# A hybrid decoder layer on one core: routing in two batches, one tile's transposes in the scores' banks, and half of the first expert's gate and up products at the end of the cross-attention

## The chip, the cores and the metric

One core of a Trainium2 chip (trn2) runs the whole program in one launch. The metric is device time in microseconds (us), lower is better. The kernel before has a median of 984.9 us over 3 runs (980.77 to 986.08).

## The reference

One decoder layer over 1024 positions of width 1024: a hybrid token mixer, a cross-attention into 256 memory rows and a grouped mixture of experts, each followed by a LayerNorm of `alpha * x + f(x)`. The change lies between the last two.

```python
def memory_cross_attention(x, mem, wq, wk, wv, wo):      # 4 heads of 128
    q = (x @ wq).reshape(b, s, XA_HEADS, XA_DIM)
    ...
    p = jax.nn.softmax(sc, axis=-1).astype(v.dtype)
    return jnp.einsum('bhsm,bmhd->bshd', p, v).reshape(b, s, XA_W) @ wo

def grouped_moe(x, router_w, router_bias, w_gate, w_up, w_down):
    scores = jax.nn.sigmoid(t @ router_w)                # 16 experts in 4 groups of 4
    biased = scores + router_bias                        # group score: its best two; best group; its best two experts
    ...
    for e in range(N_EXPERTS):
        h = jax.nn.silu(t @ w_gate[e]) * (t @ w_up[e])   # 1024 -> 256
        y = y + combine[:, e:e + 1] * (h @ w_down[e])    # 256 -> 1024
```

## The kernel before, in words

The program is a row of blocks (`project`, `prepare`, `attend`, `cross_attend`, `experts`, and `overflow`, which does work only if an expert is full). In each block every engine has its own hand-written list of instructions; engines wait for each other only by semaphores, and a block ends when all engines have come to its end. The 1024 positions are 8 tiles of 128 rows (NT = 8), and a row of 1024 is turned in KD = 8 pieces of 128.

**cross_attend.** TensorE goes through the tiles t = 0 to 7 in a software pipeline: the queries of tile t (24 products of 512 columns: high and low parts, three each for 8 pieces), in their midst the turned probabilities of tile t-1 (`turn_probs`), then `values(t-1)`, the turned queries, from t = 3 on the turned rows of the normalized tile t-3 (`turn_x2`, into the banks `x_tps`), `scores(t)`, the router's `logits(t-3)` and `outputs(t-1)`, 24 products of 512 columns into `x_acc`. ScalarE (the block `scalar`) copies turned data from the banks back (`xprobT`, `x2T`), takes the exponentials, and the high part of the values (`ohi`); VectorE takes the low part (`olo`), the maxima, the residual and the norm of a tile (`residual`, `norm`), with a reciprocal root from GpSimd between the two.

**Routing.** `rank_experts` makes scores of the logits and ranks the experts of a group, `choose` picks the group and the two experts, `place` (TensorE, a few narrow products) counts how many tokens before a token chose its expert, and `number` makes slot numbers of these counts, a 0/1 matrix `in_first` per tile that says which rows go to expert 0, and the slots for the scatter. It goes in three batches of tiles, `BATCHES`: 0 to 3, 4 and 5, 6 and 7. GpSimd then scatters each tile's rows by two indirect DMAs into `slot_rows` in DRAM (16 in all; that of tile 0 stands ahead of its share in the last tile's norm). For expert 0 the rows are not fetched back: `first_rows(t)` multiplies each tile by `in_first` in TensorE, summed over all 8 tiles in four banks, and ScalarE copies the four banks to `xgT` (`xgT_made`).

**experts.** For each of 16 experts of CAP = 176 slots TensorE multiplies gate and up (two halves m = 0, 1 of 128 hidden columns, gate and up each, 8 products a half and part), turns the next expert's rows (`turn`), and multiplies down (24 products). ScalarE takes the silu, VectorE the product, the high and low parts and the sum with the rows. SyncE waits at the start of the block until all 16 scatters have landed (`rows_scattered`), then fetches the rows of experts 0 and 1 (two DMAs each, of 128 and 48 rows), and then the down weights of expert 1 and the gate and up weights of expert 2. VectorE's list opens with clears, the low part of expert 0's down weights and then, before the first product of expert 0, the slot fields of expert 0's fetched rows (`dve.wait_ge(rows_loaded[0], 32)`).

```python
            sp.wait_ge(k.rows_scattered, 16 * 2 * NT)
            sp.wait_ge(fields_cleared, 2)
            for e in range(2):
                fetch(e * CAP, e)
```

## Time and profile before

| | us |
|---|---|
| median of 3 runs (lowest, highest) | 984.9 (980.77, 986.08) |
| the profiled execution, by its own time | 989.0 |
| its span | 987.2 |
| TensorE busy in the span | 951.2 (96%) |
| VectorE, ScalarE, GpSimd busy | 592.8, 350.8, 196.8 |
| mean granted TensorE clock | 0.986 |

The profile is of one execution, so sums made from its rows stand against 989.0 us, which is 4.1 above the median of the runs. "Busy" of TensorE counts matmuls, whose ends are modelled; weight loads overlap them. In a timeline a line is start, duration, engine, source line, operation and output<-inputs, and in brackets how long the engine stood idle before it and what released it. A matmul in fp32 shows as two instructions (x16 for 8 products). The chain of waits gives for each piece the time from its start to the start of what it released.

### The profile page before, as it was taken

To read this page: it belongs to the slowest core of one execution; us is meant where nothing else is said; L and a number is where in the kernel's file an instruction comes from. 1 tells how busy PE (TensorE), PEld (TensorE's weight loads), DVE (VectorE), ACT (ScalarE), POOL (GpSimd) and SP (SyncE) were. 2 spreads that over 40 slices of the span, in tenths; PEclk is the share of its full clock that TensorE was granted. 3 is DMA by queue.
4 is the path that set the end of the run, shared out by engine and by line. 5 is a ranking of instruction groups with operands and counts; after the bars stand their busy time and mean duration, and the time that the engine had idled before them with its cause. 6 is when DMAs were issued, how large, how long until landed. Compare 5 with 4: busy or idle time off the path is not lost. (4 is left out here: it accounts for less than half of the span.)

```text
span 987.2 us, 15735 instructions
## 1 busy us (share of the span) xinstructions
PE 951.2 (96%) x5687; PEld 805.0 (82%) x5687; DVE 592.8 (60%) x1279; ACT 350.8 (36%) x737; POOL 196.8 (20%) x256
## 2 busy tenths in 40 slices
PE   7999999999999999999999999999999999999995
PEld 6899888677767888788877888889879888888984
DVE  6744341487676776655575554567534476767676
ACT  6123031243376555410024333231232344444342
POOL 0012100121142220012220000004300134343435
PEclk9999999899999999999999999998999999999998
DMA  9122010000699500620116000044788888989872
GB/s 310 56 86 86 1 65 1 1 1 1 234 414 395 182 24 22 211 109 1 52 38 211 3 1 1 1 171 166 266 272 291 270 302 278 314 303 328 305 277 94
DMA packets 67278, 151.60 MB, mean 154 GB/s; under 512 B 8720, under 2 KB 16144, under 8 KB 67216
## 3 DMA queue, kind: packets, MB, share of 16 engines
q1 hardware_dynamic: 59920, 133.82, 38.9%
q0 software_dynamic: 7296, 16.95, 4.5%
q8 instruction: 39, 0.64, 0.2%
q14 instruction: 23, 0.19, 0.1%
HBM read 107.62 MB, written 52.03 MB: 162 GB/s over the span
## 5 line engine op out<-in xcount | busy, mean ns | idle before, releaser
L1970 PEld LDWEIGHTS h_ps<-xgT,e_gate_up 128*128 128x128 f32 x1024 | 155.6, 192 | 4.5 <-issue 2.2
L1970 PE MATMUL h_ps<-xgT,e_gate_up 128*128 128x176 f32 x1024 | 157.1, 315 | 2.2 <-DVEq L2078 2.2
L262 PE MATMUL unit_ps<-whi,xhi 128*128 128x512 f32 (+1 forms) x256 | 98.1, 383 | 6.2 <-DVE wlo L294 6.2
L263 PE MATMUL unit_ps<-wlo,xhi 128*128 128x512 f32 (+1 forms) x256 | 98.0, 383 | 0.0
L264 PE MATMUL unit_ps<-whi,xlo 128*128 128x512 f32 (+1 forms) x256 | 97.9, 383 | 0.0
L262 PEld LDWEIGHTS unit_ps<-whi,xhi 128*128 128x128 f32 x256 | 48.7, 190 | 14.0 <-DVE xlo L338 6.2
L2113 DVE SCALAR_TENSOR_TENSOR z<-y_ps,slot_weight,x_rows 128x512 f32<-128x512 f32 (+1 forms) x64 | 45.6, 746 | 23.7 <-PE y_ps L1984 21.0
L264 PEld LDWEIGHTS unit_ps<-whi,xlo 128*128 128x128 f32 x256 | 48.6, 190 | 7.8
L263 PEld LDWEIGHTS unit_ps<-wlo,xhi 128*128 128x128 f32 x256 | 48.6, 190 | 7.5
L1982 PE MATMUL y_ps<-e_dn_hi,h_hi 128*128 128x512 f32 (+1 forms) x128 | 52.1, 407 | 1.2 <-DVE z L2113 1.1
L1984 PE MATMUL y_ps<-e_dn_hi,h_lo 128*128 128x512 f32 (+1 forms) x128 | 50.2, 392 | 0.0
L1983 PE MATMUL y_ps<-e_dn_lo,h_hi 128*128 128x512 f32 (+1 forms) x128 | 50.1, 391 | 0.0
L2094 DVE TENSOR_TENSOR h<-silu_g,h_ps 128x176 f32<-128x176 f32 x32 | 10.6, 332 | 55.2 <-ACT silu_g L2021 55.2
L2021 ACT ACTIVATE silu_g<-h_ps 128x176 f32<-128x176 f32 x32 | 10.2, 317 | 92.4 <-PE h_ps L1970 85.1
L1026 PE MATMUL o_ps<-prob_T,mla_v 128*64 128x128 f32 x576 | 38.5, 278 | 4.6 <-DVE prob_T L1158 2.2
L1026 PEld LDWEIGHTS o_ps<-prob_T,mla_v 128*64 128x64 f32 x576 | 30.9, 136 | 14.6 <-DVE prob_T L1158 8.8
L2037 ACT ACTIVATE ln_junk<-z,z_neg_mean 128x1024 f32<-128x1024 f32 (+1 forms) x24 | 27.6, 1149 | 41.2 <-DVE z_neg_mean L2068 37.9
L1009 PE MATMUL t_ps<-constants,prob 128*128 128x128 f32 x288 | 41.2, 279 | 0.6 <-DVE prob_T L1158 0.4
L2048 DVE TENSOR_TENSOR e_dn_lo<-e_down_raw,e_dn_hi 128x512 fp32r<-128x512 f32 x64 | 39.7, 677 | 0.8 <-ACT e_dn_hi L2010 0.8
L1082 ACT ACTIVATE prob_T<-t_ps 128x128 f32<-128x128 f32 (+3 forms) x48 | 20.9, 435 | 51.1 <-PE t_ps L1009 51.1
L1158 DVE COPY prob_T<-t_ps 128x512 f32<-128x512 f32 (+3 forms) x48 | 29.7, 619 | 14.0 <-PE t_ps L1009 13.9
L1888 POOL COPY slot_weight<-x_rows 128x2 f32 (+1 forms) x16 | 11.8, 738 | 130.9 <-PE rowsT_ps L1953 66.9
(342 smaller groups left out, 2167.9 us busy)
## 6 DMA issues: line engine op xcount, KB each, us to landing
e_gate_up<-w_gu SPq DMA_DIRECT2D x16, 2048.0 KB, 10.7
e_down_raw<-w_dn SPq DMA_DIRECT2D x16, 1024.0 KB, 5.3
slot_rows<-zeros SPq DMA_DIRECT2D x22, 522.0 KB, 6.3
slot_sums<-zeros SPq DMA_DIRECT2D x22, 512.0 KB, 6.3
x_rows<-slot_rows SPq DMA_DIRECT2D x16, 522.0 KB, 4.5
slot_sums<-z SPq DMA_DIRECT2D x16, 512.0 KB, 4.4
wraw<-w_in SPq DMA_DIRECT2D x24, 256.0 KB, 4.6
xraw<-xT SPq DMA_DIRECT2D x16, 256.0 KB, 5.0
```

The costliest lines, as they stand in the source:

```text
L262: pe.matmul(o, hi, whi[:, s, 0:w], start=(s == 0), stop=False)
L263: pe.matmul(o, hi, wlo[:, s, 0:w], start=False, stop=False)
L264: last = pe.matmul(o, lo, whi[:, s, 0:w], start=False, stop=(s == KD - 1))
L1009: last = pe.transpose(tps[:, j, m * P:(m + 1) * P], prob[:, u % 2, j, m * P:(m + 1) * P], ident)
L1026: last = pe.matmul(ops[r, i % 2, (h // 2) * P:(h // 2 + 1) * P], k.v[:, m, h * MV:(h + 1) * MV], src, start=(m == 0), stop=(m == i))
L1158: dve.tensor_copy(probT[:, v % 2, 0, 0:(z - a) * P], tps[:, 0, 0:(z - a) * P]).then_inc(pT_copied, 1)
L1970: end = pe.matmul(hps[:, m, gu * CAP:(gu + 1) * CAP], gate_up[:, b, s, w], xT[:, s, :], start=(s == 0), stop=(s == KD - 1))
L1982: pe.matmul(out, hi, dn_hi[:, b, w, :], start=(f == 0), stop=False)
L1983: pe.matmul(out, hi, dn_lo[:, b, w, :], start=False, stop=False)
L1984: return pe.matmul(out, lo, dn_hi[:, b, w, :], start=False, stop=(f == 1))
L2048: dve.tensor_tensor(dn_lo[:, b, s, :], dn_raw[:, s, :], dn_hi[:, b, s, :].bitcast(f32), ALU.subtract).then_inc(dn_lo_done, 1)
L2113: dve.scalar_tensor_tensor(z[c][:, f], yps[r, BANK[u], :], wgt[r, b, c:c + 1], rows[b][r, c, f], ALU.mult, ALU.add, accum_out=zsum[r, c, j ...
```

## The change

- The routing goes in two batches, tiles 0 to 4 and 5 to 7. `rank_experts` is cut in two: `score_experts` (scores and bias) and the ranking. For the first batch only the scoring stays before the last tile's `olo`; the ranking comes behind it. GpSimd's scatters are 1, 4 and 3 tiles of two DMAs each, where they were 1, 3, 2 and 2.
- The pass t = 8 of TensorE is written out: `turn_x2(5)` comes ahead of `values(7)` and goes into the scores' banks `x_sps`, `logits(5)` follows, then three quarters of `outputs(7)`, `place(0)`, and the last quarter. ScalarE copies `x2T` of tile 5 before `ohi`.
- `first_rows` are placed anew around `place(1)`; the overflow's count comes before `first_rows(7)`.
- TensorE computes the half m = 0 of expert 0's gate and up (`first_gate`) at the end of the stage, into the banks of `x_tps`, which `experts` now uses as its `h_ps`. The same half is left out behind the block's start.
- SyncE fetches the rows of expert 1 before those of expert 0.

```diff
-    BATCHES = [(0, 4), (4, 6), (6, 8)]
+    BATCHES = [(0, 5), (5, 8)]
...
+                if t == NT - 3:
+                    pe.wait_ge(exps, XH * NT)
+                else:
+                    pe.wait_ge(pT_taken, min(NT, t + 3))
+                bank = sps if t == NT - 3 else tps
...
+            def first_gate():
+                pe.wait_ge(k.gu_loaded[0], 16)
+                for gu in range(2):
+                    for s in range(KD):
+                        if gu == 0 and s % 2 == 0:
+                            pe.wait_ge(k.xgT_made, s // 2 + 1)
+                        last = pe.matmul(tps[:, 0, gu * CAP:(gu + 1) * CAP], k.e_gu[:, 0, s, gu * DE:gu * DE + P], k.xgT[:, s, :],
+                                         start=(s == 0), stop=(s == KD - 1))
+                last.then_inc(k.gu_sum, 1)
...
+            turn_probs(NT - 1)
+            turn_x2(NT - 3)
+            values(NT - 1)
+            logits(NT - 3)
+            outputs(NT - 1, range(0, 3))
+            place(0)
+            outputs(NT - 1, range(3, XH))
             turn_x2(NT - 2)
...
             first_rows(1, range(KD))
+            first_rows(2, range(0, 4))
             turn_x2(NT - 1)
-            first_rows(2, range(0, 4))
+            first_rows(2, range(4, KD))
             logits(NT - 1)
-            first_rows(2, range(4, KD))
-            place(1)
             first_rows(3, range(KD))
             first_rows(4, range(KD))
-            first_rows(5, range(0, 4))
-            place(2)
-            first_rows(5, range(4, KD))
+            place(1)
+            first_rows(5, range(KD))
             first_rows(6, range(KD))
-            first_rows(7, range(KD))
             pe.wait_ge(ov_made, 1)
             pe.matmul(qps[0:1, 480:481], ovsum[:], ones[:, 0:1], start=True, stop=True).then_inc(ov_sum, 1)
+            first_rows(7, range(KD))
+            first_gate()
...
                 if t == NT:
+                    rank_experts(0)
                     choose(0)
...
                 if t == NT - 1:
-                    rank_experts(0)
+                    score_experts(0)
             norm(NT - 1)
+            score_experts(1)
             rank_experts(1)
             choose(1)
             number(1)
-            rank_experts(2)
-            choose(2)
-            number(2)
...
-            scatter(0, [1, 2, 3])
-            scatter(1, [4, 5])
-            scatter(2, [6, 7])
+            scatter(0, [1, 2, 3, 4])
+            scatter(1, [5, 6, 7])
...
-            for e in range(2):
+            for e in (1, 0):
                 fetch(e * CAP, e)
...
-                for m in range(2):
+                for m in range(1 if isinstance(e, int) and e == 0 else 0, 2):
```

TensorE's list behind the turned probabilities of the last tile, before:

```order
L1347 MATMUL x_tps<-constants,xprob 128x128 x8
L1359 MATMUL x_ops<-xprobT,xv 128x128 x8
L1369 MATMUL x_tps<-constants,x_72 128x128 x8
L1380 MATMUL x_qps<-router_w,x2T 128x16 x8
L1392 MATMUL x_sps<-selected_b,up_to 128x64
L1395 MATMUL x_sps<-selected_b,ones 128x48
```

The same place now (`x_72` is the tiles' rows, `xprob` the probabilities, `selected_b` the routing's choice):

```order
L1349 MATMUL x_tps<-constants,xprob 128x128 x8
L1375 MATMUL x_sps<-constants,x_72 128x128 x8
L1361 MATMUL x_ops<-xprobT,xv 128x128 x8
L1386 MATMUL x_qps<-router_w,x2T 128x16 x8
L1415 MATMUL x_acc<-xwo_hi,xoT_hi 128x512
```

The turned rows stand between the probabilities and the values, and 18 of the 24 output products (x_acc) now stand ahead of the place products.

TensorE's list at the end of the stage and the start of `experts`, before:

```order
L1421 MATMUL x_acc<-in_first_expert,x_72 128x176 x2
L1484 MATMUL x_qps<-ones,over_sum 1x1
L1274 UNCONDITIONAL_BRANCH
L1946 UNCONDITIONAL_BRANCH
L1970 MATMUL h_ps<-xgT,e_gate_up 128x176 x32
L1951 MATMUL rowsT_ps<-constants,x_rows_7357 128x128 x8
```

The same place now:

```order
L1428 MATMUL x_acc<-in_first_expert,x_72 128x176 x2
L1446 MATMUL x_tps<-xgT,e_gate_up 128x176 x16
L1275 UNCONDITIONAL_BRANCH
L1968 UNCONDITIONAL_BRANCH
L1992 MATMUL x_tps<-xgT,e_gate_up 128x176 x16
L1973 MATMUL rowsT_ps<-constants,x_rows_7308 128x128 x8
```

Half of the 32 gate and up products of expert 0 have moved ahead of the two branches, which are the end of one block and the start of the next.

VectorE's list where the last tile's low part stands, before:

```order
L1602 TENSOR_SCALAR rank<-rank 128x64
L1603 TENSOR_TENSOR picked<-rank,biased 128x64
L1604 TENSOR_REDUCE group_sum<-picked 128x16
L1666 TENSOR_TENSOR xoT_lo<-x_ops,xoT_hi 128x512
L1585 TENSOR_TENSOR group_beats<-group_sum 128x4x3
```

The same place now (`xoT_lo` is the low part, `beats` and `rank` the ranking):

```order
L1614 TENSOR_SCALAR neg_exp<-neg_exp 128x80
L1615 RECIPROCAL score<-neg_exp 128x80
L1616 TENSOR_TENSOR biased<-score,router_bias 128x80
L1689 TENSOR_TENSOR xoT_lo<-x_ops,xoT_hi 128x512
L1604 TENSOR_TENSOR beats<-biased 128x20x3
```

The ranking has moved from before the low part to behind it, and the batch is 80 columns wide (5 tiles of 16) where it was 64.

## Rows read from the trace of the kernel before

**Rows 1.** Windows: us, PE, PEld, DVE, ACT, POOL busy, clock, DMA share, GB/s.

```profile
659.30:676.20 16.90, 14.68 (x78) 12.41 (x77) 13.62 (x50) 2.83 (x4) 2.03 (x3) 0.80 0.06 23
668.00:672.00 4.00, 4.00 (x10) 3.13 (x11) 3.79 (x9) 0.02 (x1) 0.00 (x0) 0.50 0.02 4
702.30:718.70 16.40, 13.16 (x82) 12.69 (x81) 6.32 (x19) 5.23 (x10) 2.40 (x6) 0.90 0.82 268
718.70:960.00 241.30, 240.18 (x1480) 209.53 (x1480) 151.51 (x322) 96.92 (x201) 69.69 (x90) 1.00 0.87 295
```

**Rows 2.** Chain of waits from the last output products to expert 1's rows.

```profile
674.22 0.24 PE x_acc L1409
...
703.22 4.18 DMA slot_rows<-x,slots
707.42 0.34 SPq L1846
...
708.74 8.21 DMA x_rows<-slot_rows
```

**Rows 3.** Timeline of TensorE (PE), tile 5's logits to expert 1.

```profile
665.47 2.32 PE L1380 MATMUL x_qps<-router_w,x2T 128*128 128x16 f32 x16 [1.11 <-ACT x2T L1498]
...
683.77 1.04 PE L1369 MATMUL x_tps<-constants,x 128*128 128x128 f32 x8
...
685.92 1.96 PE L1380 MATMUL x_qps<-router_w,x2T 128*128 128x16 f32 x16
...
691.63 1.36 PE L1421 MATMUL x_sps<-in_first_expert,x 128*128 128x176 f32 x8
...
694.01 1.36 PE L1421 MATMUL x_sps<-in_first_expert,x 128*128 128x176 f32 x8
...
704.49 11.44 PE L1970 MATMUL h_ps<-xgT,e_gate_up 128*128 128x176 f32 x64 [2.17 <-DVEq L2078]
...
718.64 0.50 PE L1982 MATMUL y_ps<-e_dn_hi,h_hi 128*128 128x512 f32 x1
...
724.31 9.71 PE L1970 MATMUL h_ps<-xgT,e_gate_up 128*128 128x176 f32 x64
```

**Rows 4.** Timeline of VectorE (DVE), routing, norms and the start of experts.

```profile
662.27 0.14 DVE L1595 TENSOR_SCALAR neg_exp<-neg_exp 128x64 f32<-128x64 f32 x1
...
665.41 0.69 DVE L1666 TENSOR_TENSOR xoT_lo<-x_ops,xoT_hi 128x512 fp32r<-128x512 f32 x1
...
668.53 1.28 DVE L1576 SCALAR_TENSOR_TENSOR ln_tmp<-x,ln_mv,ln_g 128x1024 f32<-128x1024 f32 x1
...
673.77 0.16 DVE L1639 TENSOR_SCALAR x<-slots 128x4 f32<-128x4 int32 x1
676.35 1.22 DVE L1565 SCALAR_TENSOR_TENSOR x<-x,x_acc 128x1024 f32<-128x1024 f32 x1 [2.42 <-PE x_acc L1411]
...
680.15 1.28 DVE L1576 SCALAR_TENSOR_TENSOR ln_tmp<-x,ln_mv,ln_g 128x1024 f32<-128x1024 f32 x1 [1.02 <-POOL ln_rs L1750]
...
691.39 0.17 DVE L1595 TENSOR_SCALAR neg_exp<-neg_exp 128x32 f32<-128x32 f32 x1
...
698.24 0.16 DVE L1639 TENSOR_SCALAR x<-slots 128x2 f32<-128x2 int32 x1
...
712.01 0.16 DVE L2051 TENSOR_TENSOR slot_is_high<-x_rows,slot_number 128x2 f32<-128x2 f32 x1 [1.87 <-DMA x_rows<-slot_rows]
...
713.03 0.34 DVE L2096 TENSOR_TENSOR h_lo<-h,h_hi 128x176 fp32r<-128x176 f32 x1 [0.41 <-ACT h_hi L2024]
```

**Rows 5.** Timeline of GpSimd (POOL): scatters and the norm's share.

```profile
674.90 1.24 POOL L1731 DMA_INDIRECT slot_rows<-x,slots  x1 [11.60 <-DVE x L1639]
676.45 0.97 POOL L1731 DMA_INDIRECT slot_rows<-x,slots  x1 [0.30 <-issue]
...
699.20 1.18 POOL L1731 DMA_INDIRECT slot_rows<-x,slots  x1 [2.15 <-DVE x L1639]
```

**Rows 6.** Timeline of SyncE's queue: the load behind the fetches.

```profile
710.23 0.38 SPq L1857 DMA_DIRECT2D e_down_raw<-w_dn  x1
```

More of the change, by code:

```diff
@@ L1366, in turn_x2 @@
                     pe.wait_ge(x2_copied, t)
-                pe.wait_ge(pT_taken, min(NT, t + 3))
+                if t == NT - 3:
[3 more added lines that the diff above has]
+                bank = sps if t == NT - 3 else tps
                 for j in range(KD):
-                    last = pe.transpose(tps[:, j // 4, (j % 4) * P:(j % 4 + 1) * P], x1[:, t, j * P:(j + 1) * P], ident)
+                    last = pe.transpose(bank[:, j // 4, (j % 4) * P:(j % 4 + 1) * P], x1[:, t, j * P:(j + 1) * P], ident)
                 last.then_inc(x2_t, 1)
@@ L1397, in place, with outputs @@
                 last.then_inc(placed, 1)
-            def outputs(t):
+            def outputs(t, parts=range(XH)):
                 pe.wait_ge(o_lo, t + 1)
@@ L1405, in outputs @@
                     pe.wait_ge(taken, t)
-                for s in range(XH):
+                for s in parts:
                     for j in range(2):
@@ L1411, in outputs @@
                         last = pe.matmul(o, olo[:, s, :], k.xwo_hi[:, s, c], start=False, stop=(s == XH - 1))
-                last.then_inc(summed, 1)
+                if parts[-1] == XH - 1:
+                    last.then_inc(summed, 1)
             def first_rows(t, chunks):
@@ L1431, in memory_values @@
                     last.then_inc(v_sum, 1)
+            def first_gate():
[7 more added lines that the diff above has]
+                last.then_inc(k.gu_sum, 1)
             turn(0)
             memory_values(0)
-            for t in range(NT + 1):
-                if t < NT:
-                    queries(t, range(4))
+            for t in range(NT):
+                queries(t, range(4))
                 if t:
                     turn_probs(t - 1)
-                if t < NT:
-                    queries(t, range(4, KD))
+                queries(t, range(4, KD))
                 if t:
@@ L1445, in _ @@
                     memory_values(1, range(0, 1))
-                if t < NT:
-                    turn_queries(t)
+                turn_queries(t)
                 if t == 0:
@@ L1453, in _ @@
                     turn_x2(t - 3)
-                if t < NT:
-                    scores(t)
+                scores(t)
                 if t >= 3:
@@ L1461, in _ @@
                     memory_values(1, range(2, KD))
-                if t == NT:
-                    place(0)
                 if t:
                     outputs(t - 1)
+            turn_probs(NT - 1)
[5 more added lines that the diff above has]
+            outputs(NT - 1, range(3, XH))
             turn_x2(NT - 2)
@@ L1513, in _ @@
                     act.activation(probT[:].rearrange(flat), tps[:].rearrange(flat), ACT.Copy).then_inc(pT_taken, 1)
+                if t == NT:
+                    copy_x2(t - 3)
                 if t < NT:
@@ L1597, in rank_experts @@
                 link(dve.tensor_tensor(bia[:, t, :], score[:, t, :], over(rb[:, None, :], [P, hi - lo, NE]), ALU.add))
+            def rank_experts(n):
+                lo, hi = BATCHES[n]
+                t = slice(lo, hi)
                 v = bia[:, t, :].rearrange("p t (g e) -> p (t g) e", e=EG)
@@ L1800, in experts @@
     dn_hi_done, dn_lo_done = k.sem("dn_hi_done"), k.sem("dn_lo_done")
-    gsum, silu, hmul, hhi_done, hlo_done = k.sem("gu_sum"), k.sem("silu_done"), k.sem("h_mul"), k.sem("hhi_done"), k.sem("hlo_done")
+    gsum, silu, hmul, hhi_done, hlo_done = k.gu_sum, k.sem("silu_done"), k.sem("h_mul"), k.sem("hhi_done"), k.sem("hlo_done")
     ysum, z_made, z_stored, held, held_sp = (k.sem(x) for x in ("y_sum", "z_made", "z_stored", "held", "held_sp"))
@@ L1830, in is_one_of_last @@
         return isinstance(e, int) and e >= NE - count
-    with nc.psum_tensor("rowsT_ps", [P, 3, 512], f32) as tps, nc.psum_tensor("h_ps", [P, 2, 512], f32) as hps, \
+    hps = k.gate_ps
+    with nc.psum_tensor("gate_room", [P, 2, 512], f32), nc.psum_tensor("rowsT_ps", [P, 3, 512], f32) as tps, \
             nc.psum_tensor("y_ps", [P, 3, 512], f32) as yps, nc.Block(no_gpsimd_drain=True) as block:
```

14 lines of the change are left out of this document (8 added, 6 removed).

## The prediction

> **What bounds the kernel now.** I read the windows first: behind the cross-attention TensorE works 240.18 of 241.30 us at full clock [rows 1], so whatever delays it there lasts to the end, and whatever starts it earlier is kept. The two stretches with idle time that the change touches are 659.3 to 676.2 (14.68 of 16.90 busy, mean clock 0.80) and 702.3 to 718.7 (13.16 of 16.40, clock 0.90) [rows 1]. The chain of waits says which one counts. It does not run through TensorE's products just before the second stretch: it comes from VectorE's last slots (made at 698.4), through GpSimd's last four scatters, the last of which starts at 703.22 and lands 4.18 us later, SyncE's four fetch issues from 707.42 on, and 8.21 us until expert 1's rows are there at 716.95 [rows 2, 4, 5]. Then TensorE turns them and starts down at 718.64 [rows 3]. So the number to work out is when down starts; all behind it follows.
>
> **The output products (a gain that does not carry).** Before, TensorE pauses twice for 1.11 us, ahead of values(7) and, as the row shows, ahead of logits(5) [rows 3], and then the clock is granted at 0.50, the lower level (1.2 GHz), while outputs(7) runs [rows 1]: it ends at 676.2. Now the turning of tile 5 (0.9) falls into the first pause, the copy of it lies beside values(7), and the second pause goes. Values(7) starts at 661.4 as before and takes 2.05, logits 1.7: 665.2. With small pauses I expect the clock to hold, so 24 products of 0.23 (one is 0.24 [rows 2]) take 5.5, and place(0), 0.2, stands among them: 671.0, or 5.2 us earlier.
>
> VectorE can't follow. The ranking now stands behind the low part. The low part starts at 664.2, when ScalarE has its high part (1.2 earlier than the 665.41 of before). From it to tile 6's norm VectorE took 668.53 - 665.41 = 3.1, and now the ranking of five tiles on top: scoring and ranking four took 665.41 - 662.27 = 3.1 [rows 4], of which I put 1.0 on the scoring and 2.3 on ranking five. The norm of tile 6 starts at 669.6, 1.1 later. Norm and numbering took 673.93 - 668.53 = 5.4 for four tiles, so 5.7 for five: slots at 675.3, and the last residual there, not at 671.0; before it was at 676.35 [rows 4]. GpSimd took 1.0 us from the slots to tile 0's first scatter and was through with the second at 677.42, 3.5 after the slots [rows 4, 5]. Now that is 678.8, while the variance is ready 2.8 after the residual, at 678.1. So the root waits 0.7 behind the scatters, and the last norm starts at 679.9 against 680.15 [rows 4]. Of 5.2 us some 0.3 is left.
>
> **The second batch.** The last norm takes 2.6 (682.5); TensorE is free then and turns tile 7 at once, where before it came to it at 683.77 [rows 3]. Turning 0.9, half a first_rows (1.2, which covers ScalarE's copy), logits 1.9: VectorE has it at 686.8. A batch of two took 691.39 to 698.40, 7.0 us; one of four 3.1 + 2.5 + 2.7 = 8.3 [rows 4]. Three are 7.7, between the two: slots at 694.5, 3.9 earlier than before. But GpSimd then has six scatters, not four. Before it started 0.8 after the slots and 4.0 lay between the first and the fourth [rows 2, 5]; six make 6.6. Last start 694.5 + 0.8 + 6.6 = 701.9, landed 706.1 against 707.40. **Gain on the chain: 1.3 us**, of 3.9.
>
> **The half of gate and up.** Place(1) waits for nothing new, but first_rows(5) waits for its matrix, 0.8 behind the numbering's start at 692.2: 693.0, a pause of 1.3. Three tiles of 2.4 (694.01 - 691.63 [rows 3]) and the count: 700.4. The half takes 9.71 / 2 = 4.85 [rows 3]: 705.3. The block ends when the last engine does, so this replaces GpSimd's 704.2 as the barrier, and TensorE resumes at 705.6 (before 704.49). That is 0.5 ahead of the landing at 706.1, so SyncE is not held up. The other half takes 4.85, not its share of 11.44: before, after 2.17 idle, the clock fell for the first half [rows 3]. It ends at 710.5.
>
> **The fetches.** They start at 706.2, not 707.42. The first pair (718 KB) took 4.5 us to land when nothing was ahead of it (VectorE went on at 712.01 [rows 4]), the second until 716.95, 9.5 after the first issue. Now expert 1's pair is first: 710.7, turned by 712.4. Expert 0's is second, and VectorE has it ahead of all products of expert 0; before, from landing to h_lo's start took 1.1 and 0.34 for itself [rows 4], so down starts 1.45 after it. When does it land? The issue of the down weights, 1 MB, came 2.8 us after the first fetch's [rows 6]; now ScalarE's split, which follows the block's start, puts it 5.3 after. Bounds for the second pair are thus 6.7 (one DMA more than the first pair, nothing behind it slowing it) and 9.5 (as now). I take 8.0, the middle, since the next load, 2 MB of gate and up weights for expert 2, now goes out right behind the down weights where before it came at 716. Expert 0's rows land at 714.2 and down starts at 715.65, 3.05 earlier than before.
>
> The Trainium skill ("DMA: Bandwidth & Descriptors", section Queues, rings and completion order) says that on each DMA engine descriptors are consumed in ring order. By that the loads issued behind cannot slow the pair, the 9.5 would stay, and down would start at 717.15, 1.5 earlier. The trace does not decide: the second pair's last piece took 8.21 us with the load behind it, though the first pair took 4.5.
>
> **The clock at the new pause.** From 712.4 to 715.65 TensorE has nothing to do, 3.2 us. After 2.17 idle before, the clock fell and the next 64 products took 11.44, not 9.71 [rows 3]: 1.7. I charge 1.55 here, a little less, since part of a fall can lie in the pause. **Sum: 3.05 - 1.55 = 1.5 us earlier.** Against 989.0 of the profiled execution that is 987.5; the median of the runs is 4.1 below, so I forecast 984.9 - 1.5 = 983.4. Bounds: 5.6 gained (second pair after 6.7, ScalarE's silu ready, no fall and 1.2 more from terms above) to 1.5 lost (pair after 9.5 and a fall of 3.0, the cost of the long low stretch in outputs(7), 8.4 where 5.5 is usual).
>
> **Edits of no cost.** The banks shared with `experts` (the first gate waits only for tile 7's copy, 15 us earlier). The gate weights of expert 0 were sent for at the last queries and have long landed. The count ahead of first_rows(7): VectorE has it 0.8 after the slots, at 695.3.
>
> **Rivals.** (a) *The early outputs carry through.* If VectorE's ranking or GpSimd's two scatters cost less than I add up, the last norm follows outputs(7), and 3 to 5 us more come down the chain: 5 us in all at the least, 979.9. For it speaks that both pauses and the low clock go for certain; against it the residual at 675.3, which is VectorE's own sum of work. 0.15. (b) *Nothing reaches down.* By ring order the second pair lands after 9.5, and with the fall of 1.5 the gain is zero: 984.9. For it: expert 0's pair is the one that VectorE needs first, and it has been made second. 0.25. (c) *Slower: the half of gate and up holds the block's end.* TensorE comes to the block's end with 0.5 us of slack. If the pause of 1.3 at 693.0, with the turning and the pauses ahead of it, brings the lower clock, the rest of first_rows and the half lose 1.7 to 3; from 0.5 on the block starts later than the scatters land, the fetches at 707.4 to 708.6, and with the loss of 1.5 behind the fetches nothing is left: 1 to 2.5 slower, 986.4 at the middle. Against it: gate and up ended at 715.9, expert 1's rows came at 716.95, and after that pause of 1.0 the 24 products of down took 724.31 - 718.64 = 5.7, as at full clock [rows 3]. 0.15. That the change does not do what it says is excluded by the lists of instructions.
>
> **The numbers.** My forecast's own case (0.5 to 4.5 gained) has 0.45, (a) 0.15, (b) 0.25, (c) 0.15. The runs of before spread over 5.3 us, so I add 2 us on each side: 978.5 to 987.5 leaves out the far ends of (a) and (c). A difference under 0.5% (4.9 us) is about what a measurement of this kernel can't tell from none. Faster by more takes (a) in full: 0.17. Slower by more takes a shift that no case here has: 0.04. Within: 0.79.
>
> **What the profile after would show.** Outputs(7) at full clock and ended near 671; the last residual near 675.3, released by VectorE's own order and not by TensorE; the last root behind tile 0's scatters; six scatters in a row with the last landing near 706; the first gate's 32 instructions in 4.85; down of expert 0 at about 715.7, held by VectorE's wait for expert 0's rows, and a lower clock behind it. I am wrong if down starts before 714 or after 718, or if the time behind it, 268.5 us from down's start to the span's end, changes by more than 1.

## The result and the profile after

The changed kernel was slower. Over 19 runs of each the medians are 985.96 and 981.4 us, ratio 1.0046 (95% interval 1.0031 to 1.006); 12 later runs gave 1.0014 (0.9996 to 1.0033). The two intervals hardly meet, so a difference of 0.003 between two single ratios is little to build on, and I go by means over all runs where there are several: 986.1 (31 runs of the changed kernel) and 983.4 (193 of before), a loss of 2.7 us. I had forecast 1.5 us less than before. One run of e13 and one of e16 below are left out as outliers (1225.61 and 5446.77 us).

| | before, recorded | before, second trace (e1) | changed |
|---|---|---|---|
| time of the profiled run | 989.0 | 979.2 | 985.9 |
| span | 987.2 | 977.4 | 984.1 |
| mean granted clock | 0.986 | 0.994 | 0.992 |
| last tile's turned probabilities (start) | 659.29 | 655.13 | 655.95 |
| expert 1's gate and up (start) | 724.31 | 716.39 | 721.77 |
| **stretch between the two** | **65.0** | **61.3** | **65.8** |

The start of the stretch differs by 3 to 4 us between the traces although nothing ahead of it was changed; so I compare places by their distance from it, and call the stretch S. TensorE in the changed kernel (timeline: start, duration, what; idle time before it and its releaser in brackets):

```profile
655.95 1.03 PE L1349 MATMUL x_tps<-constants,xprob 128*128 128x128 f32 x8
656.82 1.04 PE L1375 MATMUL x_sps<-constants,x 128*128 128x128 f32 x8
658.10 2.05 PE L1361 MATMUL x_ops<-xprobT,xv 128*128 128x128 f32 x16 [0.24 <-ACT xprobT L1530]
659.99 1.86 PE L1386 MATMUL x_qps<-router_w,x2T 128*128 128x16 f32 x16
...
669.19 1.09 PE L1375 MATMUL x_tps<-constants,x 128*128 128x128 f32 x8 [1.52 <-DVE x L1596]
...
679.38 1.09 PE L1375 MATMUL x_tps<-constants,x 128*128 128x128 f32 x8 [1.13 <-DVE x L1596]
...
690.20 1.46 PE L1428 MATMUL x_sps<-in_first_expert,x 128*128 128x176 f32 x8 [1.46 <-DVE in_first_expert L1655]
...
697.75 4.94 PE L1446 MATMUL x_tps<-xgT,e_gate_up 128*128 128x176 f32 x32
704.26 5.01 PE L1992 MATMUL x_tps<-xgT,e_gate_up 128*128 128x176 f32 x32 [1.57 <-DVEq L2100]
711.00 1.09 PE L1973 MATMUL rowsT_ps<-constants,x_rows 128*128 128x128 f32 x8 [1.73 <-DMA x_rows<-slot_rows]
...
714.58 0.47 PE L2004 MATMUL y_ps<-e_dn_hi,h_hi 128*128 128x512 f32 x1 [1.86 <-issue]
...
721.77 9.71 PE L1992 MATMUL x_tps<-xgT,e_gate_up 128*128 128x176 f32 x64
```

The two pauses of 1.11 ahead of values(7) and logits(5) [rows 3] are 0.24 and none, as meant. But TensorE has six others: three while VectorE is late, one at the block's start, and two ahead of down. And down, 24 products, takes 721.77 - 714.58 = 7.2 us, not 5.7: windows of the changed kernel (the third number from the end is the granted clock):

```profile
709.30:711.00 1.70, 0.00 (x0) 0.00 (x1) 0.61 (x2) 1.18 (x2) 0.00 (x0) 1.00 0.76 209
712.70:714.60 1.90, 0.04 (x2) 0.05 (x1) 1.03 (x5) 0.55 (x2) 0.70 (x3) 1.00 1.03 387
714.60:718.00 3.40, 3.40 (x9) 2.25 (x10) 0.70 (x4) 3.24 (x8) 0.23 (x1) 0.59 0.99 344
```

TensorE idles twice at full clock, and when its work begins, the clock is at the lower level (1.2 GHz) for most of the next 3.4 us. VectorE, GpSimd and SyncE's queue in the changed kernel, their timelines:

```profile
660.89 0.69 DVE L1689 TENSOR_TENSOR xoT_lo<-x_ops,xoT_hi 128x512 fp32r<-128x512 f32 x1 [0.85 <-ACT xoT_hi L1540]
...
672.15 1.21 DVE L1584 SCALAR_TENSOR_TENSOR x<-x,x_acc 128x1024 f32<-128x1024 f32 x1
...
676.72 1.28 DVE L1595 SCALAR_TENSOR_TENSOR ln_tmp<-x,ln_mv,ln_g 128x1024 f32<-128x1024 f32 x1 [1.80 <-POOL ln_rs L1772]
...
683.87 0.19 DVE L1614 TENSOR_SCALAR neg_exp<-neg_exp 128x48 f32<-128x48 f32 x1 [4.54 <-ACT neg_exp L1519]
...
691.52 0.16 DVE L1662 TENSOR_SCALAR x<-slots 128x3 f32<-128x3 int32 x1
...
704.08 0.11 DVE L2099 MEMSET x_rows<- 128x20 f32 x2 [8.56 <-PEq L1275]
...
713.11 0.16 DVE L2073 TENSOR_TENSOR slot_is_high<-x_rows,slot_number 128x2 f32<-128x2 f32 x1 [3.21 <-DMA x_rows<-slot_rows]
```

```profile
674.76 0.97 POOL L1753 DMA_INDIRECT slot_rows<-x,slots  x1 [0.30 <-issue]
675.74 0.28 POOL L1771 TENSOR_SCALAR ln_mv<-ln_mv 128x1 f32<-128x1 f32 x1
...
692.48 1.18 POOL L1753 DMA_INDIRECT slot_rows<-x,slots  x1 [4.63 <-DVE x L1662]
...
699.04 0.96 POOL L1753 DMA_INDIRECT slot_rows<-x,slots  x1 [0.30 <-issue]
```

```profile
704.27 3.22 SPq L1868 DMA_DIRECT2D x_rows<-slot_rows  x4
710.00 0.38 SPq L1879 DMA_DIRECT2D e_down_raw<-w_dn  x1
710.49 0.44 SPq L1882 DMA_DIRECT2D e_gate_up<-w_gu  x1
```

The same places in the second trace of before, an undisturbed run (no low clock anywhere in S), TensorE, VectorE, GpSimd and SyncE:

```profile
661.32 1.96 PE L1380 MATMUL x_qps<-router_w,x2T 128*128 128x16 f32 x16 [1.11 <-ACT x2T L1498]
...
697.71 9.79 PE L1970 MATMUL h_ps<-xgT,e_gate_up 128*128 128x176 f32 x64 [2.17 <-DVEq L2078]
709.07 1.09 PE L1951 MATMUL rowsT_ps<-constants,x_rows 128*128 128x128 f32 x8 [1.58 <-DMA x_rows<-slot_rows]
```

```profile
669.68 1.21 DVE L1565 SCALAR_TENSOR_TENSOR x<-x,x_acc 128x1024 f32<-128x1024 f32 x1
...
674.26 1.28 DVE L1576 SCALAR_TENSOR_TENSOR ln_tmp<-x,ln_mv,ln_g 128x1024 f32<-128x1024 f32 x1 [1.80 <-POOL ln_rs L1750]
...
691.45 0.16 DVE L1639 TENSOR_SCALAR x<-slots 128x2 f32<-128x2 int32 x1
```

```profile
696.43 0.96 POOL L1731 DMA_INDIRECT slot_rows<-x,slots  x1 [0.30 <-POOLq L1274]
```

```profile
700.68 2.40 SPq L1846 DMA_DIRECT2D x_rows<-slot_rows  x4
```

Counted from the start of S, the undisturbed before against the changed kernel: last residual 14.6 and 16.2; last norm 19.1 and 20.8; last slots 36.3 and 35.6; last scatter 41.3 and 43.1; first fetch 45.6 and 48.3; down 55.6 and 58.6; end of S 61.3 and 65.8. Against a run that is not itself disturbed, the new last pass gains nothing and makes the last norm 1.6 later, two batches win 2.4 back (0.8 ahead at the last slots), and the six scatters lose 2.5. The block's start loses 1.0 more, and the low clock 1.5.

One undisturbed trace is the best case of before, as the recorded one is its worst. Seven traces with the old last pass and no filled pauses exist (the two above, e3, e9, e14, e17, e18). Their last residual lies at 14.5 to 14.6 in three, at 15.5 and 15.7 in two, at 17.0 and 17.1 in two; their last scatter starts at 42.4 on average. The changed kernel has 16.2 and 43.1 every time. So against before as it usually runs, the new pass and the two batches together start the last scatter 0.7 later.

### The profile page after: what moved, and what is told of

It is laid out like the page before. It is cut to its first block and busy times, and to the rows that moved or that the text cites. A ratio compares the mean times of both kernels' runs of the same rounds, so it can differ in the third digit from the quotient of the medians.

```text
span 984.1 us, 15687 instructions
## 1 busy us (share of the span) xinstructions
PE 944.5 (96%) x5682; PEld 800.1 (81%) x5682; DVE 588.0 (60%) x1241; ACT 350.8 (36%) x737; POOL 195.7 (20%) x256
## 5 line engine op out<-in xcount | busy, mean ns | idle before, releaser
L1992 PEld LDWEIGHTS x_tps<-xgT,e_gate_up 128*128 128x128 f32 x992 | 149.2, 190 | 4.1 <-PEq L1980 1.8
L1992 PE MATMUL x_tps<-xgT,e_gate_up 128*128 128x176 f32 x992 | 150.7, 313 | 1.6 <-DVEq L2100 1.6
L1026 PEld LDWEIGHTS o_ps<-prob_T,mla_v 128*64 128x64 f32 x576 | 31.1, 137 | 14.6 <-DVE prob_T L1158 8.8
L2059 ACT ACTIVATE ln_junk<-z,z_neg_mean 128x1024 f32<-128x1024 f32 (+1 forms) x24 | 27.6, 1150 | 41.3 <-DVE z_neg_mean L2090 38.0
L2116 DVE TENSOR_TENSOR h<-silu_g,x_tps 128x176 f32<-128x176 f32 x32 | 10.6, 332 | 53.0 <-ACT silu_g L2043 53.0
L2043 ACT ACTIVATE silu_g<-x_tps 128x176 f32<-128x176 f32 x32 | 10.1, 317 | 89.9 <-PE x_tps L1992 82.6
L2032 ACT ACTIVATE e_dn_hi<-e_down_raw 128x512 fp32r<-128x512 f32 x64 | 35.2, 637 | 8.3 <-DVE ln_tmp L2107 8.3
```

Of the source, the lines that this page charges most:

```text
L1026: last = pe.matmul(ops[r, i % 2, (h // 2) * P:(h // 2 + 1) * P], k.v[:, m, h * MV:(h + 1) * MV], src, start=(m == 0), stop=(m == i))
L1992: end = pe.matmul(hps[:, m, gu * CAP:(gu + 1) * CAP], gate_up[:, b, s, w], xT[:, s, :], start=(s == 0), stop=(s == KD - 1))
L2032: act.activation(dn_hi[:, b, s, :], dn_raw[:, s, :], ACT.Copy).then_inc(dn_hi_done, 1)
```

## The experiments

Theory A was that the half of gate and up at the stage's end holds the block's end and costs the time. Theory B was that the recorded trace of before was no usual run, and the rest of the change costs. S is from each kernel's one trace; the ratios are to before, with 12 runs each of the kernel (11 in e13 and e16).

| | edit | S | ratio (95%) |
|---|---|---|---|
| e1 | before, unchanged | 61.3 | 1.0007 (0.9987 to 1.0028) |
| e2 | changed, without the half | 63.3 | 0.9999 (0.998 to 1.0018) |
| e3 | before, with the half | 66.5 | 1.0047 (1.0026 to 1.0068) |
| e4 | changed, fetches 0, 1 | 66.5 | 1.0034 (1.0014 to 1.0053) |
| e5 | changed, fetches unhooked | 64.8 | 1.0014 (0.9994 to 1.0033) |
| e6 | changed, pauses ahead of down filled | 63.8 | 1.0005 (0.9982 to 1.0027) |
| e7 | before, new last pass | 66.5 | 1.0014 (0.9991 to 1.0037) |
| e8 | e7, residual first | 65.4 | 0.9994 (0.9975 to 1.0013) |
| e9 | before, half done twice | 63.8 | 1.0017 (0.9995 to 1.0039) |
| e10 | before, three pauses filled | 66.0 | 1.0038 (1.0015 to 1.006) |
| e11 | e8, three pauses filled | 65.6 | 1.0035 (1.0013 to 1.0058) |
| e12 | changed, unchanged | 67.2 | 1.0014 (0.9996 to 1.0033) |
| e13 | changed, late reading | 62.0 | 0.9998 (0.9975 to 1.0021) |
| e14 | before, fetches 1, 0, late reading | 63.7 | 0.9981 (0.9958 to 1.0004) |
| e15 | e2, late reading | 63.0 | 1.001 (0.9993 to 1.0027) |
| e16 | e8, fetches 1, 0, late reading | 62.6 | 1.0001 (0.9982 to 1.002) |
| e17 | before, fetches 1, 0 | 62.8 | 0.996 (0.9938 to 0.9981) |
| e18 | e14 again | 59.4 | 0.9971 (0.9944 to 0.9998) |

**e1, the kernel before.**

> The kernel before, unchanged. Both theories: ratio 1.000 within 0.002. Theory A (the block's end): its trace looks like the recorded one, 59.3 us from the last tile's turned probabilities to the first down product and 65.0 to the second expert's gate. Theory B (the recorded profile of before was no usual run, 989.0 against a median of 981.4): outputs(7) runs at the full clock, nothing is lost further up, and the 65.0 us are 3 to 4 shorter, so there was less to gain than I summed.

Both traces of before have the 1.11 pauses; in the recorded one the clock fell behind them and behind the block's start, in this one it did not, and S is 3.8 shorter. Over the 12 runs a mean clock of 0.994 goes with 979.2 and one of 0.985 with 988.1. So B's first part holds: the recorded run was a slow sample, though not the only one (e14's trace has the same low clock in outputs(7)).

**e2, no half at the stage's end; e3, the half alone.**

```diff
-            first_rows(7, range(KD))
-            first_gate()
+            first_rows(7, range(KD))
...
-                for m in range(1 if isinstance(e, int) and e == 0 else 0, 2):
+                for m in range(2):
```

> The changed kernel with both halves of expert 0's gate and up behind the block's start, as before; all else of the change stays. Theory A: the half at the stage's end made TensorE the last engine at the block's end; without it the block starts at least 3 us earlier, the fetches start right after the last scatter lands (1 us earlier), TensorE has no long pause ahead of down, and the time is 2.5 to 3.5 us under the changed kernel, ratio to before 1.001 to 1.002. Theory B (the rest of the change, such as six scatters in a row, is what costs): within 1 us of the changed kernel, ratio 1.004 to 1.005.

> The kernel before with the half of gate and up at the stage's end as the only edit. Theory A: the block starts 4 to 5 us later and so do the fetches (by 2 to 3, as the last scatter's landing no longer decides), 2 to 4 us slower than before, ratio 1.002 to 1.004. Theory B: ratio 0.999 to 1.001.

e2 has a mean of 983.8, 2.2 (give or take 1.3) under the changed kernel's and as fast as before, and e3, before with only the half moved, is slower than before with its whole interval (mean 987.9, more than I gave it). So A holds: the half costs about 2 us in the changed kernel. Two parts of what I expected did not come. The fetches of e2 start 0.6 earlier than the changed kernel's, not 1; and B is not out, since e2 also has the swapped fetches, which e17 shows to be a gain. TensorE in e3's trace:

```profile
697.64 5.04 PE L1441 MATMUL x_tps<-xgT,e_gate_up 128*128 128x176 f32 x32
704.25 5.01 PE L1984 MATMUL x_tps<-xgT,e_gate_up 128*128 128x176 f32 x32 [1.57 <-DVEq L2092]
712.82 1.97 PE L1965 MATMUL rowsT_ps<-constants,x_rows 128*128 128x128 f32 x8 [3.56 <-DMA x_rows<-slot_rows]
...
722.70 9.71 PE L1984 MATMUL x_tps<-xgT,e_gate_up 128*128 128x176 f32 x64
```

The second half is done at 709.26 and TensorE then idles 3.56 us for expert 1's rows, with the turning at half speed (1.97, usually 1.09) behind it. Before, the two halves together covered that wait.

**e4, the old order of the fetches.** `for e in (1, 0)` back to `for e in range(2)` in the changed kernel.

> The changed kernel with the rows of expert 0 fetched first, as before. If the order (1, 0) is a cost by itself (VectorE is held by expert 0's rows, TensorE pauses 1.9 us ahead of down and the clock falls, 1.5 us): 1 to 1.5 us under the changed kernel. If it is a help: down waits for expert 1's rows, lands 2 us later and must be turned, 0.5 to 1.5 us over it. Theory A and B both allow either; the ratio to before is 1.003 to 1.006.

One pause of 3.27 in place of 1.73 and 1.86; the time is not told apart from the changed kernel's (means 986.3 and 986.1). With the half moved, either order leaves a hole of 3.3 to 3.6 in all.

**e5, fetches at the end of the cross-attention's list.** The clears that they wait for move with them, to the end of VectorE's list; the four lines in `experts` are gone.

```diff
+            sp.wait_ge(k.rows_scattered, 16 * 2 * NT)
+            sp.wait_ge(k.fields_cleared, 2)
+            for e in (1, 0):
+                for c in range(2):
+                    ...
```

> The changed kernel, half of gate and up included, but the four fetches of rows stand at the end of the cross-attention's SyncE list (and the clears they wait for at the end of VectorE's), so that they start when the last scatter lands and not when the next block starts. Block's end theory: in the changed kernel's trace the last scatter starts at 699.04 and lands 4.2 later, at 703.2, and the fetches start at 704.27; so they start 1.0 to 1.2 us earlier, all behind them moves with them, and the pauses ahead of down get shorter by as much: 1 to 2.5 us under the changed kernel, ratio to before 1.002 to 1.0035. If the fetches are not what down waits for: within 0.5 us of the changed kernel, 1.0045.

S is 1.0 shorter, but the mean, 985.6, is only 0.5 under the changed kernel's and not told apart from it. The fetches start about 0.5 earlier, not the 1.0 to 1.2 that I expected. The block's end now comes behind SyncE's last issue (over at 708.38), TensorE's pause moves there, and it has a low clock behind it (6.69 for a half that takes 5.01):

```profile
709.92 6.69 PE L1998 MATMUL x_tps<-xgT,e_gate_up 128*128 128x176 f32 x32 [4.31 <-DVEq L2072]
```

**e6, the pauses ahead of down filled with products of no use.**

```diff
+                    if isinstance(e, int) and e == 0:
+                        fill(5)
                     turn(1 - b, h(32, 32 * (1 + b)))
+                    if isinstance(e, int) and e == 0:
+                        fill(6)
```

> The changed kernel with 5 products of no use in TensorE's pause ahead of turning expert 1's rows and 6 in the pause ahead of expert 0's down, 128x176 each into a bank that down overwrites. They measure what the lower clock behind the pauses costs: if it is a cost of its own, the 24 down products take 5.6 us and not 7.2, and the time is 1 to 1.5 us under the changed kernel, ratio 1.003. If it only looks like one (down waits for something else anyway): no difference, 1.0045.

In its trace down takes 5.7 and S is 2.1 shorter; the mean clock of its runs is 0.9937 against 0.9916. The mean time, 985.2, is 0.8 under the changed kernel's, give or take 1.9, so the price of the low clock (1.5 in a trace) is seen in traces and not in the times alone.

**e7, the new last pass alone; e8, the last residual ahead of number(0).** e7 is before with the last pass of the change's own diff (tile 5's rows turned into the scores' banks, ranking behind the low part, place(0) in the fourth quarter) and three batches kept. e8's diff is against e7; it also puts tile 6's logits ahead of first_rows(0).

```diff
-            first_rows(0, range(0, 4))
             logits(NT - 2)
-            first_rows(0, range(4, KD))
+            first_rows(0, range(KD))
...
-                if t == NT:
-                    number(0)
                 if t:
                     residual(t - 1)
+                if t == NT:
+                    number(0)
...
-                if t == NT - 1:
-                    scatter(0, [0])
...
-            scatter(0, [1, 2, 3])
+            scatter(0, [0, 1, 2, 3])
```

> The kernel before with only the last pass's part of the change: tile 5's turned rows in the scores' banks ahead of values(7), the ranking of the first batch behind the low part, place(0) in the fourth quarter of outputs(7). Three batches, no half of gate and up, fetches as before. Outputs(7) always runs at the full clock; runs of before in which it does not lose 1.3 (e3's trace) to 2.9 us (the recorded trace). VectorE's own order sets the last residual in both. So 0.5 to 2 us under before, ratio 0.998 to 0.9995. If the two batches are what made e2 no slower than before, and this part is worth nothing: 1.000.

> e7, and the last tile's residual stands ahead of number(0) in VectorE's list, its root ahead of tile 0's scatters in GpSimd's, and logits(6) ahead of first_rows(0). My sum: the last norm 2.2 us earlier, the last scatter 1.3 us earlier than in an undisturbed run of before, ratio 0.996 to 0.998. If something else sets the last slots (the two last batches' ranking is 15 us of VectorE in a row and starts only behind the last norm, so it should follow): as e7.

e7 missed. Its trace has the early outputs, and then TensorE waits 2.04 ahead of tile 7's turning, the logits take 3.43 instead of 1.96 and gate and up 11.46. place(1) stands behind these logits in TensorE's list, and VectorE, which is on the chain, waits 4.19 us for it (0.52 in e1):

```profile
686.92 0.19 DVE L1638 SCALAR_TENSOR_TENSOR fits<-x_qps,selected 128x32 f32<-128x32 f32 x1 [4.19 <-PE x_qps L1399]
```

So the pause went to where the chain runs, and the last slots come at 41.4 (36.3 in e1). e8 missed too (I had expected 0.996 to 0.998): its residual comes at 12.9 and its norm at 18.2, earlier than in any trace of before, but a pause of 1.11 ahead of tile 6's logits is followed by a low clock (3.54), and the last slots come at 39.5.

**e9, the half done twice.** As e3, the result of the first unused, and all 32 products behind the block's start.

> The kernel before with the 16 products of the half at the stage's end as in e3, their result unused, and all 32 products behind the block's start as well: the half is computed twice. If work behind the block's start is free there (TensorE waits for expert 1's rows anyway), the saving of e3 is worth nothing, and doing the half twice costs no more than moving it: ratio within 0.002 of e3's 1.0047. If the moved half did save 4.9 us behind the start, this is 4 to 5 us slower than e3, ratio 1.009 to 1.010.

```profile
702.11 9.79 PE L1983 MATMUL x_tps<-xgT,e_gate_up 128*128 128x176 f32 x64 [1.57 <-DVEq L2091]
711.73 1.04 PE L1964 MATMUL rowsT_ps<-constants,x_rows 128*128 128x128 f32 x8
```

Doing the work twice costs less than moving it: no pause ahead of the turning, the full clock, and a mean of 985.0 against e3's 987.9 (2.9, give or take 2.0). The 4.9 us that the change saved behind the block's start were free. The trace also splits the cost of the half: with it at the stage's end the fetches start 1.4 later than in e1 and S is 2.5 longer (e9), and with half of the cover gone S is 2.7 longer still (e3), of which 1.1 is there before the fetches start, from a low clock in outputs(7), and the rest behind them.

**e10, e11, filled pauses at values, logits and the block's start.** e10 is before with 3, 3 and 4 products of no use ahead of values(7), logits(5) and gate and up; e11 is e8 with 3 ahead of tile 6's turning, 3 ahead of its logits and the same 4. The diff shows the last place.

```diff
+            for _ in range(4):
+                pe.matmul(yps[:, 0, 0:CAP], ident, k.g3[:, 0:CAP], start=True, stop=True)
             pe.wait_ge(k.xgT_made, 4)
```

> The kernel before with 3 + 3 + 4 products of no use in TensorE's pauses: ahead of values(7), ahead of logits(5) and at the start of the experts' block, 0.9 to 1.2 us each. If the clock's falls behind these pauses are what spreads the runs of before, and part of what the change moved about: the clock in the runs rises from 0.991 to 0.993 or more and the time is 1 to 2.5 us under before, ratio 0.9975 to 0.999. If not: 1.000 to 1.001.

> e8 with 3 products of no use ahead of the turning of tile 6, 3 ahead of its logits and 4 at the start of the experts' block. e8's trace had a low clock behind both (logits of 3.54 us, gate and up of 11.46). Clock theory: 2 to 4 us under e8 and before, ratio 0.996 to 0.998. Otherwise as e8, 0.9994.

Both are slower than before, the opposite of what I expected. The fills do what they should (gate and up 9.79), but TensorE waits longer ahead of the turning:

```profile
696.16 9.79 PE L1982 MATMUL h_ps<-xgT,e_gate_up 128*128 128x176 f32 x64
709.63 1.97 PE L1960 MATMUL rowsT_ps<-constants,x_rows 128*128 128x128 f32 x8 [3.69 <-DMA x_rows<-slot_rows]
```

The obvious reading, that a faster TensorE only waits longer for a fixed arrival, does not fit e10. Counted from S its last scatter starts at 41.3 and its gate and up at 42.6, as in e1, but expert 1's rows come at 56.1, not at 53.9. Most of that is the last scatter's landing, from the chains of waits of e1 (first line) and e10:

```profile
696.43 4.24 DMA slot_rows<-x,slots
694.88 6.16 DMA slot_rows<-x,slots
701.06 0.34 SPq L1855
```

In e11 it is 5.75 (4.20 in e8). Behind the longer pause the low clock falls on the turning (1.97 for 1.09) and on down (7.05 for 5.7), which are on the chain; that part is the moved half's mechanism. Why the scatter lands late, and whether it does so in the other runs, is open: e10's traced run took 982.7, 4.4 under the mean of its runs.

**e12, the changed kernel again.**

> The changed kernel, unchanged, on the same chip as the three above: ratio 1.003 to 1.005; the trace tells whether 65.8 us from the last tile's turned probabilities to the second expert's gate, and the low clock behind the pause ahead of down, are usual.

S is 67.2, with pauses of 1.46 and 2.23 ahead of down, and down takes 8.5. So the recorded trace of the change was no outlier. The ratio, 1.0014, came out under the 1.003 to 1.005 that I expected.

**e13 to e18, late reading and the swap.** VectorE reads expert 0's fields behind expert 0's products:

```diff
-            dve.wait_ge(rows_loaded[0], 32)
-            know_high(0, 0)
-            place(1, 0)
             steps(dve, step)
...
+                if isinstance(e, int) and e == 0:
+                    dve.wait_ge(rows_loaded[0], 32)
+                    know_high(0, 0)
+                    place(1, 0)
```

> The changed kernel, but VectorE reads the slot fields of expert 0's rows behind expert 0's products, not ahead of them, so that down does not wait for expert 0's rows. If the second pause of TensorE (1.9 to 2.2 us ahead of down) and the low clock behind it are held there by the swap of the fetches together with this order: the second pause goes, down starts 1.9 us earlier and runs at the full clock, 2.5 to 3.5 us under the changed kernel, ratio to before 0.999 to 1.0005. If the late start of the block alone is the cost: 0 to 1 us under, 1.002.

> The kernel before with expert 1's rows fetched first and the same late reading of expert 0's fields, nothing else. Expert 1's rows then land 6 to 7 us after the fetches' start, not 8.4 to 9.5, while TensorE is still at gate and up: no pause ahead of down, 1 to 2.5 us under before, ratio 0.9975 to 0.999. If the clock low behind the block's start eats it: 1.000.

> e2 (two batches, the new last pass, expert 1's rows first, both halves behind the block's start) with the late reading. In e2's trace down waited only 0.16 us, so there is next to nothing to win: within 1 us of e2, ratio 0.999 to 1.000. If it is much faster than e2, expert 0's rows held more than that trace shows.

> e8 (three batches, new last pass, last residual ahead of number(0)) with expert 1's rows first and the late reading. e8's TensorE waited 0.93 us for expert 1's rows; that pause goes. 1 to 2 us under e8, ratio to before 0.997 to 0.9985, the best of all if the two gains add.

> The kernel before with expert 1's rows fetched first as the only edit; VectorE still reads expert 0's fields ahead of expert 0's products. It tells what e14's gain came from. If the late reading is what matters: down waits for expert 0's rows, 8.8 us after the fetches' start plus 1.45, which in an undisturbed run is where it starts in the kernel before too: ratio 0.999 to 1.001. If the swap alone brings it: 0.998, as e14.

> e14 once more, on the same chip as e17: if its gain is real the ratio is again 0.997 to 0.999, and with e14's the interval lies under 1. If e14 was luck with the clock: 1.000.

e17 is before with `for e in range(2)` of the fetches changed to `for e in (1, 0)`; e14 and e18 add the late reading to it.

In e13 down follows the turning at once and at full clock, S is 3.8 shorter than the changed kernel's, and the mean is 3.1 lower, with the late start of the block left in:

```profile
714.01 1.09 PE L1973 MATMUL rowsT_ps<-constants,x_rows 128*128 128x128 f32 x8 [1.37 <-DMA x_rows<-slot_rows]
...
715.66 0.50 PE L2004 MATMUL y_ps<-e_dn_hi,h_hi 128*128 128x512 f32 x1
...
721.34 9.71 PE L1992 MATMUL x_tps<-xgT,e_gate_up 128*128 128x176 f32 x64
```

The mean of e13 is that of e15 (983.0 both): with the late reading the moved half costs nothing that can be told (give or take 1.8), which points to the wait for expert 0's rows as the way in which it cost its time in the changed kernel.

e14 and e18 are the version that beats both kernels: before, with the fetches swapped and the late reading (mean 980.6 over 24 runs, 2.8 under before; e18's ratio lies under 1 with its interval, e14's just not). In e18's trace expert 1's rows are there when gate and up end, and nothing waits (in e14's neither, but there outputs(7) and gate and up have a low clock, and S is 63.7):

```profile
697.45 9.79 PE L1970 MATMUL h_ps<-xgT,e_gate_up 128*128 128x176 f32 x64 [2.18 <-DVEq L2078]
707.07 1.04 PE L1951 MATMUL rowsT_ps<-constants,x_rows 128*128 128x128 f32 x8
...
708.66 0.50 PE L1982 MATMUL y_ps<-e_dn_hi,h_hi 128*128 128x512 f32 x1
...
714.30 9.71 PE L1970 MATMUL h_ps<-xgT,e_gate_up 128*128 128x176 f32 x64
```

e17 was a miss: the swap alone, which I had put at no gain, gave 0.996 (mean 981.4), not told apart from e18 on the same chip; its trace has a pause of 2.04 ahead of down. The fetch order of the change is thus a gain by itself, and the late reading's share in e14 is open. e15 and e16 both came out slower than I expected (0.999 to 1.000 and 0.997 to 0.9985).

Read together, these runs show a second loss that e2 alone hides. e15 is the changed kernel without the half and with the late reading; e14 and e18 have the old last pass and the three batches instead (and with them the old places of first_rows), and are 2.4 us faster (give or take 1.4) on the same chip. Without the late reading it is the same: e17 is 2.4 under e2 (give or take 1.7, on two chips; the ratios, 0.996 and 0.9999, differ by as much). So against before the change is a sum of three parts: about 2.0 won by the swap, about 2.4 lost by the new last pass with the two batches, about 2.2 lost by the moved half. Theory B's second part holds beside A. The traces show two things that go with it: the last scatter 0.7 later, and the clock in gate and up behind the block's start. Of ten traces with both halves only there and no fill, all five with the new pass (e2, e7, e8, e15, e16) have it low (11.35 to 11.46 us) and two of the five with the old one (9.79 in the rest). That the new pass causes this is not shown.

## Why the prediction was wrong

In the recorded run's time down was to start at 715.65 and started at 717.9: 2.3 later, of which the fetches' start is 1.4 and the landing of expert 0's rows 0.8. So of the 3.05 to be won there (2.99, by the two starts) 0.7 was left, and the low clock behind it, 1.5 as charged, made the stretch 0.8 longer than the recorded one, 65.8 against 65.0. The other half of the error is that this 65.0 was no usual value. My signs of being wrong were both set against that run, and neither showed: down at 717.9 lies between 714 and 718, and behind it there are 269.5 us, 1.0 more than 268.5. The time itself lies in the stated range, which is that wide for the spread of the runs; the direction was wrong.

**The base was a disturbed run.** I summed against the recorded run (989.0) and took its 8.4 us for outputs(7) as the kernel's own. Of my first term, 5.2, the clock in outputs(7) is 2.9, which was not there to be won in an undisturbed run; and I compared the last residual with 676.35, which that low clock had made late. By the second trace VectorE had it at 14.6 behind the start of S, not 17.1, and the change made it 16.2. My own numbers for VectorE were right (forecast 675.3 in the recorded run's time, measured 672.15 + 3.34 = 675.5; last norm 679.9 and 680.1; last slots 694.5 and 695.0, read the same way), the thing they were compared with was not. The median of 3 runs beside a profiled run 4.1 above it was the sign; I noted it and went on. With the median of 19 the distance is 7.6.

**The block's end.** I took GpSimd's last scatter, over at 704.18, for the engine that released the block, with 0.3 behind it. In the changed kernel TensorE is through at 702.69 and VectorE's first clear comes at 704.08, 1.4 later. That term was short by 1.1, the half itself ended 0.7 later than forecast, and the 0.5 of slack that I had given it was not there: the fetches start at 704.27, in the recorded run's time 707.6; I had said 706.2. Counted from the start of the last scatter that is 5.2, against 4.2 before and 4.6 in e2, so 0.6 of it is the half's and 0.4 is there without it. This is what rival (c) gave (fetches at 707.4 to 708.6, and 986.4), which I held for improbable, but not for its reason: the pause ahead of first_rows(5) came (1.46), yet the granted clock was 1.00 from 689 to 703 and the half took 4.94.

**The cover.** My sum took the moved half for free: 4.85 us of it ahead of the block's end, nothing for it behind, and I asked only whether it delays the block. It was the cover of the wait for the fetched rows (e9 against e3). I had worked out the pause of 3.2 us ahead of down, and charged it 1.55; measured are 1.73 + 1.86 and 1.5. The pauses and their price were right. What was wrong is what they were set against: a gain of 3.05 at down that was 0.7, and in an undisturbed run of before a down that starts 3.0 earlier than the changed kernel's (55.6 and 58.6 behind the start of S) and at full clock.

**The last pass and the batches.** I put them at a gain of 1.3 on the chain. By e15 against e14 and e18 they lose 2.4. Against an undisturbed run the six scatters, for which I had charged 2.6 more than for four, lose 2.5, as I reckoned; the 3.9 that I had set against them at the last slots is 0.8 there. Why the loss in the means is larger than what the traces show at the last scatter (0.7 on average) is open.

**The fetches.** The first pair landed after 6.7 us, not 4.5, the second after 8.8, not 8.0. I had put it down in part to loads issued behind them. The traces don't show that: the second pair took 8.4 in e1 with the down weights issued 2.8 us behind the first fetch, 8.5 in e3 with them 5.7 behind, 8.8 in the changed kernel. The Trainium skill ("DMA: Bandwidth & Descriptors", section Queues, rings and completion order) says that on each DMA engine descriptors are consumed in ring order; these three numbers agree with that. But two other traces with the down weights 2.8 behind, the recorded one of before and e8, took 9.5, so what makes the second pair land early or late is open.

**What held.** Both pauses and the low clock in the last pass went; the count and landing of six scatters (43.1 against 41.3: later, not earlier, by the right base); the low clock behind the pause. Rival (a) fell: nothing of the early outputs came down the chain, since VectorE's ranking and numbering took their place (the residual is at 16.2; e8, which puts it first, has 12.9). Of rival (b) the second half holds, VectorE waits 3.21 us for expert 0's rows; its 9.5 us did not come, the pair took 8.8.

What stays open is how often the clock falls at each pause. Behind the two pauses of 1.11 it was low for half of outputs(7) in two of seven traces, for four or five products in two, and not at all in three. Ahead of down, behind single pauses of 3.27 to 3.69 (e3, e4, e10, e11), down took 6.9 to 7.1; behind one of 1.37 (e13), 1.58 (e1) and 2.04 (e17) it took 5.6 to 5.7. Only one or two traces per kernel exist, and the spread of the runs (a mean clock lower by 0.001 goes with about 0.8 to 1 us) is as large as the effects.

## What to carry to other kernels

Before pricing a change against a trace, check that the traced run is a usual one: its time against all runs, and its clock in the very stretch that the change touches. Work that an engine does while it would wait for a transfer anyway is free, and moving it ahead of a barrier that starts the transfer costs twice: the transfer starts later, and the wait is bare. On TensorE a bare wait can also cost clock behind it, so first look for an edit that makes the arrival earlier: the one-line swap of the fetches (e17) was worth about 2 us. And when a change of several parts comes out at nothing, try its parts one by one: e2's 0.9999 was a gain and a loss of about 2 us each.

## What was not expected of the hardware

Filling pauses with products of no use held the clock there and made the kernel slower (1.0038 and 1.0035); in both traces the last scatter landed 1.6 to 1.9 us later than in e1 and e8, for a reason that no run here shows. And a block's end is not free where TensorE comes last: 1.39 to 1.40 us lie between its last product and VectorE's first work of the next block in the changed kernel (702.69 to 704.08), e3, e9 and e12. Where GpSimd's last scatter comes last, as in e1, it is 0.14 (697.39 to 697.53), so a price read behind one engine does not hold for another.
